# A convolution's taps as 64-wide diagonals on the array's quadrants, a norm's squares summed on VectorE, and an output in four transfers

## What is computed

```python
def rmsnorm(x, w):
    y = xf * lax.rsqrt(jnp.mean(xf * xf, axis=-1, keepdims=True) + EPS)
    return (y * w.astype(jnp.float32)).astype(x.dtype)

def conformer_conv(h, w_pw1, b_pw1, w_dw, b_dw, ln_g, ln_b, w_pw2, b_pw2):
    a, gate = jnp.split(h @ w_pw1 + b_pw1, 2, axis=-1)
    y = a * jax.nn.sigmoid(gate)
    y = lax.conv_general_dilated(y, w_dw[:, None, :], window_strides=(1,),
                                 padding=[(CONV_K // 2, CONV_K // 2)], ...,
                                 feature_group_count=CONV_W) + b_dw      # CONV_K = 31
    y = jax.nn.silu(layernorm(y, ln_g, ln_b))
    return y @ w_pw2 + b_pw2
```

## Time and profile before

| | us |
|---|---|
| median of 3 runs | 2672.74 |
| lowest, highest | 2672.31, 2678.84 |
| profiled execution, its own time | 2676.76 |
| its span in the trace | 2674.8 |
| TensorE busy in the span | 2576.0 |
| VectorE busy | 1549.6 |
| ScalarE busy | 1013.2 |
| GpSimd busy | 98.5 |

### The profile page before, as it was taken

The page is one execution under the profiler, slowest core; times in us unless marked ns, Lnnn a source line. Parts: engine busy times, 40 slices in busy tenths (PEclk is TensorE's granted clock), DMA queues, the critical chain, the costliest instruction groups (busy, mean ns, idle before and its releaser), DMA issues.

```text
span 2674.8 us, 30981 instructions
## 1 busy us (share of the span) xinstructions
PE 2576.0 (96%) x12302; PEld 2047.6 (77%) x12302; DVE 1549.6 (58%) x2584; ACT 1013.2 (38%) x1556; POOL 98.5 (4%) x124
## 2 busy tenths in 40 slices
PE   8999999999999989999988998999999998999998
PEld 6887788887986667888877876788888665788886
DVE  5455676867355656646564355666653998534433
ACT  4344443434335555434344344322322214323323
POOL 0000000000000000000000000011100010000000
PEclk9999999999899999999999998999999999999999
DMA  5322336454121122333333211366642121233331
GB/s 168 111 80 85 89 99 176 150 162 130 53 87 52 56 72 71 97 93 95 91 92 115 91 59 40 121 194 194 194 132 71 56 63 32 86 96 95 97 100 47
DMA packets 283494, 266.83 MB, mean 100 GB/s; under 512 B 13283, under 2 KB 268567, under 8 KB 283351
## 3 DMA queue, kind: packets, MB, share of 16 engines
q1 hardware_dynamic: 266919, 210.33, 25.7%
q0 software_dynamic: 15024, 54.33, 6.9%
q10 hardware_dynamic: 1408, 0.20, 0.0%
HBM read 262.72 MB, written 2.10 MB: 99 GB/s over the span
## 4 chain that ended last, share of the span: by engine, by line
PE 87%; DVE 7%; issue 2%; ACT 2%; DMA 1%; ACTq 0%; POOL 0%; DVEq 0%; POOLq 0%
PE G L2209 70%; PE G L2225 7%; PE M L2277 2%; DVE Y L2040 2%; DVE S L2040 1%; PE M L711 1%; PE M L1117 1%; PE M L772 1%; PE M L782 1%; DVE w_lo L496 1%; PE M L1590 1%; PE M L2259 1%; PE M L1128 1%; PE M L1139 1%; PE M L1579 0%
## 5 line engine op out<-in xcount | busy, mean ns | idle before, releaser
L496 DVE TENSOR_TENSOR w_lo<-raw,w_hi 128x1024 fp32r<-128x1024 f32 x396 | 482.9, 1224 | 683.8 <-ACT w_hi L491 682.6
L2209 PE MATMUL G<-H_hi,w_hi 128*128 128x512 f32 (+1 forms) x2016 | 808.9, 401 | 18.1 <-DVE H_lo L359 9.6
L491 ACT ACTIVATE w_hi<-raw 128x1024 fp32r<-128x1024 f32 x396 | 417.0, 1056 | 994.2 <-PE G L2209 886.9
L2209 PE MATMUL G<-H_hi,w_lo 128*128 128x512 f32 (+1 forms) x2016 | 787.9, 391 | 0.0
L2209 PE MATMUL G<-H_lo,w_hi 128*128 128x512 f32 (+1 forms) x2016 | 787.6, 391 | 0.0
L2209 PEld LDWEIGHTS G<-H_hi,w_hi 128*128 128x128 f32 x2016 | 382.9, 190 | 121.2 <-issue 39.4
L2209 PEld LDWEIGHTS G<-H_lo,w_hi 128*128 128x128 f32 x2016 | 383.1, 190 | 80.3 <-issue 5.9
L2209 PEld LDWEIGHTS G<-H_hi,w_lo 128*128 128x128 f32 x2016 | 382.3, 190 | 80.1
L2209 PE MATMUL G<-hid_hi,w_hi 128*128 128x512 f32 x864 | 339.1, 392 | 5.8 <-DVE hid_lo L615 4.7
L2209 PE MATMUL G<-hid_lo,w_hi 128*128 128x512 f32 x864 | 338.5, 392 | 0.0
L2209 PE MATMUL G<-hid_hi,w_lo 128*128 128x512 f32 x864 | 338.3, 392 | 0.0
(11 more groups left out here) (311 smaller groups left out, 2421.4 us busy)
## 6 DMA issues: line engine op xcount, KB each, us to landing
raw<-in_w_ff SPq DMA_DIRECT2D x128, 512.0 KB
mod_w<-in_w_mod POOLq DMA_DIRECT2D x96, 512.0 KB, 4.5
raw<-in_ffn_w_up SPq DMA_DIRECT2D x176, 256.0 KB
raw<-in_ffn_w_down SPq DMA_DIRECT2D x40, 512.0 KB
raw<-in_w_in SPq DMA_DIRECT2D x28, 512.0 KB
raw<-in_mlstm_w_in SPq DMA_DIRECT2D x24, 512.0 KB
raw<-in_kv_w SPq DMA_DIRECT2D x16, 512.0 KB
raw<-in_fox_w_qg SPq DMA_DIRECT2D x16, 512.0 KB
```

What stands on the lines that cost most here:

```text
L491: act.activation(w_hi[:, j, :], raw[:, j, :], ACT.Copy).then_inc(hi_done, 1)
L496: dve.tensor_tensor(w_lo[:, j, :], raw[:, j, :], w_hi[:, j, :], ALU.subtract).then_inc(lo_done, 1)
L2209: mm = pe.matmul(G[:, 2 * p + m, 0:n], lw[:, k, ms], rh[:, t, 0:n], start=(t == 0 and q == 0), stop=(t == st["ktiles"] - 1 and q == 2), sk ...
```

## The change

Fourteen of the 31 taps go to TensorE in place of ten, and VectorE keeps 17. Each of the fourteen is a pair of 64x64 diagonals (`tap_diag` is now 64 wide) on the quadrants of the array. Seven taps read `yp`: rows 0 to 63 into columns 0 to 63 in bank 2p, rows 64 to 127 into columns 64 to 127 in bank 2p + 1. The other seven read `yp_turned`, a copy of `yp` with its partition halves exchanged, and cross over: low rows into the high columns of bank 2p, high rows into the low columns of bank 2p + 1. Four such matmuls make a round, seven rounds a block. ScalarE makes `yp_turned` after each gated product with two copies of 64 partitions, and once `taps_turned` from the tap weights; before it copies, it waits for the gated product and for tap block g - 2. GpSimd builds the diagonals in two operations of 7 x 64 elements. VectorE adds both banks (`total_low`, `total_high`) with the sum of its two accumulators between them, and clears `yp_turned` once. The ones-matmuls of the layer norm write G's bank 0.

In the first norm, VectorE adds the squares of tiles 1 to 7 onto those of tile 0 (`collected`), and TensorE runs one ones-matmul after the first stage in place of one per tile. The output goes in four transfers of 256 columns each, each as soon as its two tiles are in `x_tm`.

```diff
-PE_TAPS = 10
+PE_TAPS = 14
+HALF_TAPS = PE_TAPS // 2
...
-            sp.wait_ge(fin_c, 8)
             out_v = out.rearrange("a (b p) d -> p (a b) d", p=P)
-            sp.dma_start(out_v, x_tm[:]).then_inc(done, 16)
-            sp.wait_ge(done, 16)
+            for t in range(1, DT, 2):
+                sp.wait_ge(fin_c, t + 1)
+                part = slice((t - 1) * P, (t + 1) * P)
+                sp.dma_start(out_v[:, :, part], x_tm[:, :, part]).then_inc(done, 16)
+            sp.wait_ge(done, 64)
...
-                pe.wait_ge(cv_w, g + 1)
+                pe.wait_ge(cv_w, 2 * g + 2)
                 wait_read(pe, "p_1", g)
+                pe.wait_ge(cv_x, 2 * g + 4)
                 pe.wait_ge(cv_d, g + 1)
-                for j in range(PE_TAPS):
-                    mm = pe.matmul(M[:, 2 + p, :], tap_diag[:, p, j, :], yp[:, p, V_TAPS + j:V_TAPS + j + T],
-                                   start=(j == 0), stop=(j == PE_TAPS - 1))
+                low, high = slice(0, HP), slice(HP, P)
+                for j in range(HALF_TAPS):
+                    here, there = V_TAPS + j, V_TAPS + HALF_TAPS + j
+                    for hs, bank in ((low, 2 * p), (high, 2 * p + 1)):
+                        pe.matmul(M[hs, bank, :], tap_diag[hs, p, j, :], yp[hs, p, here:here + T], start=(j == 0),
+                                  stop=(j == HALF_TAPS - 1), skip_group_check=True)
+                    for hs, other, bank in ((low, high, 2 * p), (high, low, 2 * p + 1)):
+                        mm = pe.matmul(M[other, bank, :], tap_diag[hs, p, HALF_TAPS + j, :],
+                                       yp_turned[hs, p, there:there + T], start=(j == 0), stop=(j == HALF_TAPS - 1),
+                                       skip_group_check=True)
                 mm.then_inc(cv_pe, 1)
...
+                wait_read(act, "p_1", g)
+                act.wait_ge(cv_pe, g + 1)
+                for to, hs in ((slice(HP, P), slice(0, HP)), (slice(0, HP), slice(HP, P))):
+                    act.activation(yp_turned[to, p, PAD:PAD + T], yp[hs, p, PAD:PAD + T], ACT.Copy).then_inc(cv_x, 1)
...
                 link.wait(0)
                 if g:
-                    total(g + (-1), 1 - p)
+                    total_low(g - 1, 1 - p)
                 dve.tensor_tensor(y, y, other, ALU.add).then_inc(cv_v, 1)
+                if g:
+                    total_high(g - 1, 1 - p)
                 dve.wait_ge(cv_v, g + 1)
...
+            for t in range(DT):
+                p = t % 2
+                pool.wait_ge(cv_pe, t + 1)
+                pool.tensor_tensor(tap_diag[:, p, 0:HALF_TAPS], each,
+                                   taps[:, V_TAPS:V_TAPS + HALF_TAPS, t:t + 1].to_broadcast([P, HALF_TAPS, HP]),
+                                   ALU.mult).then_inc(cv_w, 1)
+                pool.tensor_tensor(tap_diag[:, p, HALF_TAPS:PE_TAPS], each,
+                                   turned[:, :, t:t + 1].to_broadcast([P, HALF_TAPS, HP]),
+                                   ALU.mult).then_inc(cv_w, 1)
...
             def pre_need(t):
                 if t < 4:
                     x_turn(t + 4)
-                norm_tiles("pre0", (t,))
                 pe.wait_ge(h_lo, FILL["pre0"] + t + 1)
...
             finish(first)
+            pe.wait_ge(n_ss, 7)
+            pe.matmul(M[:, 0, :], ones[:], SA[:, 0, :], start=True, stop=True).then_inc(n_ss, 1)
...
+            def collected(t):
+                dve.wait_ge(n_sq, t + 1)
+                if t >= 2:
+                    dve.wait_ge(n_ss, t - 1)
+                dve.tensor_tensor(SA[:, 0, :], SA[:, 0, :], SQ[:, t % 2, :], ALU.add).then_inc(n_ss, 1)
...
                 unscaled_dve(dve, "pre0", mix_weight, t - 2)
+                collected(t - 2)
```

More of the change, by code:

```diff
@@ L243, in build @@
         yp = at("yp", 112 * K, [P, 2, T + 2 * PAD])
-        tap_diag = at("tap_diag", 117 * K, [P, 2, PE_TAPS, P])
+        tap_diag = at("tap_diag", 117 * K, [P, 2, PE_TAPS, HP])
+        yp_turned = at("yp_turned", 125 * K, [P, 2, T + 2 * PAD])
+        taps_turned = at("taps_turned", 130 * K, [P, 8 * HALF_TAPS])
+        half_ident = at("half_ident", 131 * K, [P, HP])
         G = ctx.enter_context(nc.psum_tensor("G", [P, 4, 512], F32))
@@ L1916, in second_pe @@
             linear("p_1", H_hi, H_lo, need=from_h("odd"), behind=taps)
+            wait_read(pe, "p_1", DT - 2)
             for t in range(DT):
                 pe.wait_ge(cv_d, t + 3)
-                mm = pe.matmul(M[:, 1, :], ones[:], Y[:, t, :], start=(t == 0), stop=(t == 7))
+                mm = pe.matmul(G[:, 0, :], ones[:], Y[:, t, :], start=(t == 0), stop=(t == 7))
             mm.then_inc(cv_s, 1)
@@ L1958, in glu @@
                                bias=VT[:, ds(g + (ROW["b_pw1_2"] + 8), 1)]).then_inc(glu_a, 1)
+                wait_read(act, "p_1", g)
+                act.wait_ge(cv_pe, g + 1)
+                for to, hs in ((slice(HP, P), slice(0, HP)), (slice(0, HP), slice(HP, P))):
+                    act.activation(yp_turned[to, p, PAD:PAD + T], yp[hs, p, PAD:PAD + T], ACT.Copy).then_inc(cv_x, 1)
+            turned_taps = ROW["w_dw_2"] + 8 * (V_TAPS + HALF_TAPS)
+            for to, hs in ((slice(HP, P), slice(0, HP)), (slice(0, HP), slice(HP, P))):
+                act.activation(taps_turned[to, :], VT[hs, turned_taps:turned_taps + 8 * HALF_TAPS],
+                               ACT.Copy).then_inc(cv_x, 1)
             groups(act, "p_1", split_hi, glu)
@@ L2010, in second_dve @@
             dve.wait_ge(chunk_used, used_after("s0_down3"))
+            dve.memset(yp_turned[:], 0.0)
             link(dve.memset(yp[:], 0.0))
@@ L2016, in second_dve, with total_low, total_high @@
             mod_rest(dve, link, 1)
-            def total(g, p):
+            def total_low(g, p):
                 dve.wait_ge(cv_pe, g + 3)
-                y = Y[:, ds(g, 1), :]
-                dve.tensor_tensor(y, y, M[:, 2 + p:3 + p, :], ALU.add).then_inc(cv_d, 1)
+                y = Y[:, g, :]
+                dve.tensor_tensor(y, y, M[:, 2 * p, :], ALU.add).then_inc(cv_a, 1)
+            def total_high(g, p):
+                dve.wait_ge(cv_a, g + 1)
+                y = Y[:, g, :]
+                dve.tensor_tensor(y, y, M[:, 2 * p + 1, :], ALU.add).then_inc(cv_d, 1)
             def glu(i, p, g):
@@ L2174, in _ @@
             taps = VT[:, ROW["w_dw_2"]:ROW["w_dw_2"] + 8 * CONV_K].rearrange("p (j t) -> p j t", t=8)
-            for i in range(0, DT // 2):
-                for p in range(2):
-                    pool.wait_ge(cv_pe, i * 2 + (p + 1))
-                    pool.tensor_tensor(tap_diag[:, p], ident[:].unsqueeze(1).to_broadcast([P, PE_TAPS, P]),
-                                       taps[:, V_TAPS:CONV_K, ds(i * 2 + p, 1)].to_broadcast([P, PE_TAPS, P]),
-                                       ALU.mult).then_inc(cv_w, 1)
+            turned = taps_turned[:].rearrange("p (j t) -> p j t", t=8)
+            pool.tensor_tensor(half_ident[:], ident[:, 0:HP], ident[:, HP:P], ALU.add).then_inc(cv_h, 1)
+            pool.wait_ge(cv_h, 1)
+            pool.wait_ge(cv_x, 2)
+            each = half_ident[:].unsqueeze(1).to_broadcast([P, HALF_TAPS, HP])
+            for t in range(DT):
[7 more added lines that the diff above has]
+                                   ALU.mult).then_inc(cv_w, 1)
         @block.tensor
@@ L2468, in _ @@
             x_copy(3)
+            collected(1)
             split_lo(dve, 1)
@@ L2472, in _ @@
                 unscaled_dve(dve, "pre0", mix_weight, t - 2)
+                collected(t - 2)
                 if t in (5, 7):
                     split_lo(dve, t // 2)
-            unscaled_dve(dve, "pre0", mix_weight, 6)
-            unscaled_dve(dve, "pre0", mix_weight, 7)
+            for t in (6, 7):
+                unscaled_dve(dve, "pre0", mix_weight, t)
+                collected(t)
             modulation = modulation_steps(dve, link, 0)
```

15 lines of the change are left out of this document (8 added, 7 removed).

## The result

The changed kernel takes 2654.45 us (median of 4 runs, 2651.30 to 2656.78) where the kernel before, in the same set of runs, takes 2673.77 (4 runs, 2672.31 to 2678.84). The ratio is 0.9924, with a 95% interval of 0.9906 to 0.9941: 19.3 us less. Forecast were 2651.8 us and 20.9 us less. The profiled execution took 2651.30 us, its span 2649.5; that is 25.3 less than the span before, so 6 us of the difference between the two traces are not the change's. Where they lie has to be known before the traces are compared.

The account below looks back on a forecast made before the run. The prediction saw VectorE and TensorE both full in the convolution stage, with VectorE's trail setting its end. Terms of -17.5, -0.8 and -2.6 sum to -20.9, from 2676.76 to 2655.9 profiled, 2651.8 us as median; range 2643 to 2662.

Parts of the forecast that it names:

- The tap block and TensorE's period: Convolution stage on TensorE: four quadrants overlap fully, a block takes 6.3 us and the period becomes 17.25 us.
- VectorE's savings: Convolution stage: four fewer taps save 21.2 us, second adds cost 4.9, net -16.3; period without stall 15.91 us.
- The stalls: Convolution stage: VectorE's tap 0 operation waits out GpSimd's diagonal builds, 7.0 us in all, 1.0 less than before.
- The sign that I gave for it: Convolution stage trace: VectorE's L2034 still near 1.9 us, with GpSimd's builds ending just before it does.
- rival A: Whole kernel, everything at its better bound: VectorE free of GpSimd, no clock fall, fast output; 28.7 us gained, 2644; chance 0.15.
- The stage: Convolution stage in sum: -16.3 from VectorE's work and -1.0 from stalls give -17.3, taken as -17.5 us.
- The first norm: Kernel start: dropping four later sums from TensorE nets 2.5 us, one clock fall takes back 1.7; -0.8 us.
- The output: Kernel end: four transfers at 304 GB/s, a rate taken from loads, land at 2671.75 instead of 2674.4; -2.6 us.
- From the sum to the median: Whole kernel: profiled execution less 20.9 gives 2655.9; the runs' median, 4.0 lower than the profiled execution, gives 2651.8 us.

## Why the prediction was right, step by step

**The tap block and TensorE's period.** Right. The four quadrants overlap wholly, the block takes 6.2 us (6.3) and the period is 17.28 (17.25). What the two axes showed apart in the earlier trace rows holds for both at once.

**VectorE's savings.** Right. Taps out, second adds in: VectorE's own group without any stall is 15.77 to 15.79 us (15.91 forecast), shown where GpSimd builds nothing. The prediction set out from a period of 19.41 us, that of one group; four of the seven were 19.2.

**The stalls.** The size was right, 7.0 us, and the mechanism was wrong. I had VectorE held at TensorE's period by a build that starts when a block ends and meets tap 0: whenever it came early, it would wait for the build. In fact its period of 17.17 is its own 15.77 and two times 0.70, and the same total comes when the builds start 2 us later. The stall is 0.70 us for each build of 0.95, less what lies beside an operation that reads PSUM. That it fell so near to 17.25 was chance. The sign that I gave for it, tap 0 near 1.9 us with the builds ending just before it does, did not come: tap 0 was 0.81 us in the mean, and the rest lay on the two operations behind it. The error bears on rival A, which I gave 0.15 for "two short GpSimd operations leave a gap": starting the builds later freed nothing, and only what fell beside the gated product was free. With the builds on ScalarE the stage gains 1.9 us more, 20.1 in all and not the 22.5 of that case. I had left out that the last gated product still comes 2.4 us behind the last linear group (2193.98 against 2191.58), and that TensorE's sums behind block 7 then set the end.

**The stage.** -17.5 forecast, -18.2 measured, and 25.5 us lost where the quadrants are missing: the term that carries the sum is shown from both sides. My terms gave -17.3, and the step from there to -17.5 had no source. The 0.9 us by which the stage did better than that is about what seven periods gain when VectorE's own group is 0.14 shorter than forecast.

**Behind the stage.** The step that was missing: the norm's sums at the low clock, +1.5 us. It came in all five executions with this stage as it is, and in none of the other seven. What sets the five apart in the traces is a gap of 1.2 us ahead of tap block 7, some 15 us before the gap of 1.4 us ahead of the sums, which all twelve have. In the kernel before, the first of the two is 0.7 us, with ScalarE's builds there is none, and with the later builds it is 3.97 us and the clock falls right there. No run changed that gap alone, so that it decides is argued, not shown.

**The first norm.** The term was -0.8: 2.5 for four sums, 1.7 back for a fall of the clock. In the traces the time from the vector rows to the end of the first stage is 15.16 us with the sums on TensorE (three executions), 12.72 with the change and a clock that stays high (three), 14.2 to 14.8 with a fall (four). So the four sums are worth 2.4 us, the fall costs 1.5 to 2.1, and both terms were sized rightly. The vector rows themselves start at 29.0 to 29.9 us with the change, at 28.9 and 29.2 without, which takes a part of it back. Counted from the span's start, the first stage ends at 44.1 to 44.3 us with the sums on TensorE (46.2 in a third execution), at 41.7 to 42.7 with the change and no fall, at 43.8 to 44.1 with one: with the fall, as forecast, little is left, 0 to 0.5 us where I had 0.8. That I took the fall as given was wrong, since it came in four of seven executions. The gap was 2.1 to 4.8 us. It is not the length alone that decides: a gap of 2.12 had a fall behind it, one of 2.93 had none.

**The output.** -2.6 forecast, -2.9 and -2.8 measured. The rate was 341 GB/s where I had taken 304 from loads; the last issue ended at 2645.6, the span 3.9 us later.

**From the sum to the median.** I took the profiled execution of before as 4.0 us above its median and carried that over. The profiled execution of the changed kernel was 3.2 below its own. What the edits do adds up to 16.2 + 2.9 + 2.6 = 21.7 us without a fall of the clock at the start (up to 1.0 of it TensorE's earlier first matmul) and between 19.1 and 19.6 with one, and the medians differ by 19.3. That the forecast of 20.9 came so near owes something to luck: the stage gave more than forecast, the 1.5 us behind it were missing, and the start's term was tied to a fall that came in four of seven executions.

## What to carry to other kernels

An fp32 matmul on 64 rows and 64 columns costs the array as much time as a whole one (0.43 us a pass) unless its neighbours in the program are on the other quadrants: put four that differ next to each other, and the four take the time of one (28 matmuls in 6.2 us in place of 19.3). If GpSimd does small jobs beside a VectorE that is the bound, most of their running time is VectorE's time (0.70 of 0.95 us here), except beside VectorE's operations that read PSUM; give them to ScalarE when it has room, and look first which engine ends the stage then. And where two traces of one kernel differ by 15 us in a stretch that no edit touches, compare stretches, not spans, and look at how long the clock was low in each.

## What the hardware showed that I had not expected

- Passes on one quadrant overtake passes on another that are earlier in the program, by three or four passes and no further (block of 19.3 us, between 6.2 and the 24 of a strict sequence).
- Who waits for whom between GpSimd and VectorE can go the other way. With 1792 elements in a build (14 full diagonals), asked for in the middle of VectorE's chain, the build took 9.71 us (3.20 undisturbed): the chain's operations stayed at 0.75, and only when VectorE read PSUM did the build run. Then VectorE's next sum took 2.99 us in place of 0.68:

```profile
2106.67 9.71 POOL L2178 TENSOR_TENSOR tap_diag<-ident,VT 128x1792 f32<-128x1792 f32 x1 [38.10 <-PE M L1911]
...
2112.55 0.75 DVE L2040 SCALAR_TENSOR_TENSOR Y<-yp,VT,Y 128x512 f32<-128x512 f32 x1
2113.33 0.69 DVE L2022 TENSOR_TENSOR Y<-Y,M 128x512 f32<-128x512 f32 x1
2113.93 2.99 DVE L2044 TENSOR_TENSOR Y<-Y,S 128x512 f32<-128x512 f32 x1
```

  Why this build did not get in between two operations of the chain, as those of 448 elements did, stays open.
- Stores of 512-byte, 1 KB and 4 KB runs moved 289, 341 and 406 GB/s at full DMA share.
- The granted clock falls behind (or inside) some gaps of 2 to 5 us and not behind others of the same length, in executions of the same code; a fall cost 1.5 to 2.1 us each time.
